# One transfer each way for the diagonal blocks, the decay rows behind them, and a fifth slot for expert weights

## The reference, cut to what matters

```python
# DeltaNet, one chunk: solve with a unit lower triangular matrix, then a recurrence over chunks
A = jnp.where(strict, jnp.einsum('bhnid,bhnjd->bhnij', kb, k) * decay, 0.0)
rhs = jnp.concatenate([v * beta[..., None], kb * jnp.exp(g)[..., None]], -1)
sol = lax.linalg.triangular_solve(eye + A, rhs, left_side=True, lower=True, unit_diagonal=True)
...
def step(S, xs):
    u_n, w_n, qk_n, qd_n, kd_n, gl_n = xs
    v_new = u_n - jnp.einsum('bhcd,bhde->bhce', w_n, S)
    o = jnp.einsum('bhcd,bhde->bhce', qd_n, S) + jnp.einsum('bhij,bhje->bhie', qk_n, v_new)
    S = S * gl_n[..., None, None] + jnp.einsum('bhcd,bhce->bhde', kd_n, v_new)
    return S, o
...
# experts: top two of one group, weighted
hid = jax.nn.silu(jnp.einsum('bld,edf->blef', h, w_gate)) * jnp.einsum('bld,edf->blef', h, w_up)
y = jnp.einsum('blef,efd->bld', hid * combine[..., None].astype(hid.dtype), w_down)
```

## Time and profile before

| | |
|---|---|
| median of three runs | 1129.16 us |
| the profiled execution | 1132.07 us |
| its span, first to last instruction | 1130.3 us |
| TensorE matmuls busy | 814.6 us (72%) |
| TensorE weight loads busy | 486.4 us (43%) |
| VectorE busy | 418.0 us (37%) |
| ScalarE busy | 322.9 us (29%) |
| GpSimd busy | 280.6 us (25%) |
| chain that ended last | PE 34%, DMA 25%, GpSimd 14%, DVE 11% |

### The profile page before, as it was taken

One profiled execution on the slowest core, in us unless ns is written; L12 is line 12 of the kernel. 1 busy time (PEld: TensorE's weight loads), 2 busy tenths in 40 slices (PEclk: granted clock), 3 DMA queues, 4 the chain that ended last, 5 costly groups with the idle time before them and its releaser, 6 DMA issues.

```text
span 1130.3 us, 14986 instructions
## 1 busy us (share of the span) xinstructions
PE 814.6 (72%) x5183; PEld 486.4 (43%) x5183; DVE 418.0 (37%) x1012; ACT 322.9 (29%) x724; POOL 280.6 (25%) x684
## 2 busy tenths in 40 slices
PE   5596658999983439284979689697836944999850
PEld 0253225555541023153656566566635423555430
DVE  0318431111112850252556366464644252111105
ACT  0121313222222222242345254452631021222112
POOL 0000002333321000043626336254360001333220
PEclk8588778999987659588889698888976975999985
DMA  9997299967894982562342513424100085999942
GB/s 345 363 393 298 112 375 358 331 217 282 314 352 146 378 249 75 185 179 37 95 86 53 123 39 94 91 50 122 38 5 6 1 350 207 356 364 350 376 135 111
DMA packets 119779, 227.23 MB, mean 201 GB/s; under 512 B 43421, under 2 KB 85733, under 8 KB 105255
## 3 DMA queue, kind: packets, MB, share of 16 engines
q1 hardware_dynamic: 107232, 198.66, 51.8%
q0 software_dynamic: 8224, 22.56, 6.2%
q10 hardware_dynamic: 4263, 5.21, 1.4%
HBM read 213.25 MB, written 17.33 MB: 204 GB/s over the span
## 4 chain that ended last, share of the span: by engine, by line
PE 34%; DMA 25%; POOL 14%; DVE 11%; issue 5%; SPq 5%; ACT 4%; ACTq 1%; DVEq 0%; POOLq 0%
PE banks L607 10%; DMA h_cols<-in_w_down_dram 7%; POOL arena L982 6%; POOL arena L980 6%; PE banks L619 5%; DMA weight_ring<-in_w_mod_dram 4%; DMA arena<-h_of_tokens,row_now 3%; DMA inverted_blocks<-arena 3%; PE banks L1000 3%; DMA arena<-blocks 3%; PE banks L1714 3%; PE banks L250 2%; SPq L964 2%; PE banks L587 2%; DMA blocks<-arena 2%
## 5 line engine op out<-in xcount | busy, mean ns | idle before, releaser
L1000 PE MATMUL banks<-h_cols,weight_ring 128*128 128x512 f32 (+1 forms) x384 | 166.3, 571 | 0.9 <-ACT modulation L273 0.7
L666 DVE TENSOR_TENSOR arena<-arena,banks 128x128 f32<-128x128 f32 x42 | 12.1, 289 | 235.2 <-ACT arena L635 235.2
L250 PE MATMUL banks<-weight_ring,c_cols 128*32 128x512 f32 x384 | 62.0, 747 | 47.4 <-DMA weight_ring<-in_w_mod_dram 47.1
L1000 PEld LDWEIGHTS banks<-h_cols,weight_ring 128*128 128x128 f32 x384 | 76.0, 215 | 44.0 <-issue 37.5
L702 POOL DMA_INDIRECT y_of_tokens<-arena,place_now x42 | 42.8, 1018 | 195.9 <-ACT arena L642 195.9
L982 POOL TENSOR_TENSOR arena<-arena 128x60 f32<-128x60 f32 (+10 forms) x240 | 78.8, 328 | 18.8
L607 PE MATMUL banks<-weight_ring,arena 128*64 128x256 f32 x640 | 78.8, 403 | 6.4 <-DMA weight_ring<-in_w_down_dram 4.0
L980 POOL TENSOR_TENSOR arena<-arena 128x60 f32<-128x60 f32 (+10 forms) x240 | 78.4, 327 | 18.8
L680 POOL DMA_INDIRECT arena<-h_of_tokens,row_now x50 | 46.3, 925 | 99.4 <-DVE place_of_slot L568 49.0
L630 ACT COPY arena<-arena 64x1024 f32<-64x1024 f32 x46 | 48.1, 1045 | 77.7 <-PE banks L587 57.0
L587 PE MATMUL banks<-const,arena 64*128 64x64 f32 x352 | 57.1, 285 | 12.9 <-ACT arena L630 12.9
(11 more groups left out here) (265 smaller groups left out, 1409.2 us busy)
## 6 DMA issues: line engine op xcount, KB each, us to landing
weight_ring<-in_w_mod_dram SPq DMA_DIRECT2D x48, 1024.0 KB, 12.1
weight_ring<-in_w_gate_dram SPq DMA_DIRECT2D x16, 1024.0 KB, 7.4
weight_ring<-in_w_up_dram SPq DMA_DIRECT2D x16, 1024.0 KB, 10.4
weight_ring<-in_w_down_dram SPq DMA_DIRECT2D x16, 1024.0 KB, 12.7
weight_ring<-in_dn_w_in_dram SPq DMA_DIRECT2D x32, 512.0 KB, 6.6
arena<-in_w_gate_dram SPq DMA_DIRECT2D x8, 1024.0 KB, 12.1
arena<-in_w_up_dram SPq DMA_DIRECT2D x8, 1024.0 KB, 14.4
arena<-in_w_down_dram SPq DMA_DIRECT2D x8, 1024.0 KB, 17.9
```

The source lines that it names most:

```text
L250: mm = pe.matmul(m.ps[j * COL:(j + 1) * COL, 0, :], m.c_cols[:, k, :], w[:, j, :], start=(k == 0), stop=(k == KD - 1))
L1000: mm = pe.matmul(bank(6 + j % 2)[:, 0:CTX + SEQ - n0], head_w[h % 2][:, j, k, :], m.hT[:, k, n0:CTX + SEQ], start=(k == 0), stop=(k == KD ...
```

## The change

- A fifth slot for expert weights, in pieces: two for gate and up (in `modulation` and the second half of `h_cols`), two for down (`modulation`, `mod_sums`). It takes six DMAs instead of three. `expert_loaded` works out the count to wait for; the loop of `sp_moe` is written out for 11 experts.
- The diagonal blocks pass through two compact tiles, `N_diag` and `W_diag`. VectorE and ScalarE copy two quarters each into `N_diag`; one DMA stores it, one DMA loads `W_diag`. ScalarE copies `W_diag` onto the diagonal of `W` (`act_place_blocks`), VectorE transposes straight from `W_diag`. The DRAM layout is now system first, block second.
- `M` is loaded by one DMA whose source is repeated four times.
- SP issues `sp_along` behind `sp_blocks_in`.
- TensorE does five of eight slices of projection 1, then the keys, then the other three. ScalarE takes the squares before the pad of projection 1.
- The arguments of `N` of head x+2 move into recurrence steps 1 and 2, their exponentials to the end of the recurrence, and the third convolution into steps 0 and 1.

```diff
-EXPERT_SLOTS = 4
+EXPERT_SLOTS = 5
...
+        EXPERT_LOADS = [3, 3, 3, 3, 6]
...
+            sp.wait_ge(s("mod_spread"), QUAD * (NQ + 1))
+            sp_expert(sp, L, 4, 4)
             sp.wait_ge(s("router_meta"), L.n + 1)
...
+            for e in range(N_EXPERTS - EXPERT_SLOTS):
+                nt, tb = expert_count(sp, e)
+                sp.wait_ge(s(L.tag + "down"), tb + nt)
+                sp_expert(sp, L, e + EXPERT_SLOTS, e % EXPERT_SLOTS)
...
         def sp_blocks_out(sp, h):
-            sp.wait_ge(s("n_mat"), 2 * (h + 1))
-            for k in range(NB):
-                r = slice(k * BLK, (k + 1) * BLK)
-                sp.dma_start(n_dram[k].rearrange("s r c -> r s c"), N[h % 2][r, :, r]).then_inc(s("n_out"), 16)
+            sp.wait_ge(s("n_mat"), 3 * (h + 1))
+            sp.wait_ge(s("k_length"), 6 * (h + 1))
+            sp.dma_start(n_dram.rearrange("s k r c -> (k r) s c"), N_diag).then_inc(s("n_out"), 16)
 
         def sp_blocks_in(sp, h):
-            sp.wait_ge(s("n_out"), 16 * NB * (h + 1))
-            for g in range(4):
-                sp.dma_start(M[g * BLK:(g + 1) * BLK, :, :], n_dram.rearrange("k s r c -> (k s) r c")).then_inc(s("m_in"), 16)
-            sp.dma_start(U, n_dram.rearrange("k s (q g) c -> g (k s) q c", g=4)).then_inc(s("m_in"), 16)
+            sp.wait_ge(s("n_out"), 16 * (h + 1))
+            sp.dma_start(M, n_dram.rearrange("s k r c -> (s k) (r c)").unsqueeze(0).to_broadcast([4, BLK, BLK * BLK])
+                         ).then_inc(s("m_in"), 16)
+            sp.dma_start(U, n_dram.rearrange("s k (q g) c -> g (s k) q c", g=4)).then_inc(s("m_in"), 16)
...
         def sp_inverse_in(sp, h):
             sp.wait_ge(s("u_out"), 16 * (h + 1))
             if h >= 1:
-                sp.wait_ge(s("o_done"), h)
-            else:
-                sp.wait_ge(s("w_clear"), 2)
-            for k in range(NB):
-                r = slice(k * BLK, (k + 1) * BLK)
-                sp.dma_start(W[r, :, r], w_dram[k].rearrange("s r c -> r s c")).then_inc(s("w_base"), 16)
+                sp.wait_ge(s("v_base"), h)
+                sp.wait_ge(s("joined"), 11 * (h - 1) + 3)
+            sp.dma_start(W_diag, w_dram.rearrange("s k r c -> (k r) s c")).then_inc(s("w_base"), 16)
...
+            if h >= 1:
+                dve.wait_ge(s("n_out"), 16 * h)
+            dve.wait_ge(s("n_mat"), 3 * h + 2)
+            for k in (0, 1):
+                ins = dve.tensor_copy(N_diag[quarter(k), :, :], N[h % 2][quarter(k), :, quarter(k)])
+            ins.then_inc(s("n_mat"), 1)
...
+        def act_place_blocks(act, h):
+            act.wait_ge(s("w_base"), 16 * (h + 1))
...
+            for k in range(NB):
+                ins = act.copy(W[quarter(k), :, quarter(k)], W_diag[quarter(k), :, :])
+            ins.then_inc(s("joined"), 1)
...
         def sp_step(sp, x):
             if closed(x):
                 sp_inverse_out(sp, x)
-            if closed(x) and x + 2 < HEADS:
-                sp_along(sp, x + 2)
-            if closed(x):
                 sp_inverse_in(sp, x)
             if made(x):
                 sp_blocks_out(sp, x + 1)
                 sp_blocks_in(sp, x + 1)
+            if closed(x) and x + 2 < HEADS:
+                sp_along(sp, x + 2)
+            if made(x):
                 sp.wait_ge(s("proj"), proj_made(x + 1, 2))
...
+        V_FIRST = 5
+
         def pe_step(pe, x):
             if made(x):
-                pe_project(pe, x + 1, 1)
+                pe_project(pe, x + 1, 1, 0, V_FIRST)
                 pe_keys(pe, x + 1)
+                pe_project(pe, x + 1, 1, V_FIRST, KD)
...
-            if made(x) and x >= 0:
-                act_exp_n(act, x + 1)
...
             def beside_recur(st):
                 if made(x):
                     act_values(act, x + 1, st)
-                    if st == TT - 1:
+                    if st == TT - 2:
                         act_conv(act, x + 1, 2)
+                if st == TT - 1 and x + 2 < HEADS:
+                    act_exp_n(act, x + 2)
...
             def beside_recur(st):
-                if made(x) and st < 3:
-                    dve_conv(dve, x + 1, 2, 2 * st, min(2 * st + 2, TAPS))
-                if st == 3 and x + 2 < HEADS:
-                    dve_n_args(dve, x + 2)
+                if made(x) and st < 2:
+                    dve_conv(dve, x + 1, 2, 3 * st, min(3 * st + 3, TAPS))
+                if x + 2 < HEADS and st in (1, 2):
+                    dve_n_args(dve, x + 2, *((0, 3), (3, SYS))[st - 1])
```

More of the change, by code:

```diff
@@ new lines, in build, with gate_up, down @@
+        pieces_down = [m.mod[:, 4 * D:5 * D], m.sums.rearrange("p a n -> p (a n)")]
+        EXPERT_LOADS = [3, 3, 3, 3, 6]
+        def gate_up(slot, k):
+            if slot < EXPERT_SLOTS - 1:
+                return whole[slot].rearrange("p a (k f) -> p a k f", k=KD)[:, :, k, :]
+            return pieces[k // (KD // 2)][:, :, k % (KD // 2), :]
+        def down(slot, c):
+            if slot < EXPERT_SLOTS - 1:
+                return whole_down[slot].rearrange("p (c n) -> p c n", c=FC)[:, c, :]
+            return pieces_down[c]
@@ new lines, in sp_expert, with expert_loaded @@
+            w = w_down_flat[n * FE:(n + 1) * FE, :].rearrange("(c p) n -> p c n", p=P)
+            if slot < EXPERT_SLOTS - 1:
+                sp.dma_start(whole_down[slot].rearrange("p (c n) -> p c n", c=FC), w).then_inc(done, 16)
+            else:
+                for c in range(FC):
+                    sp.dma_start(pieces_down[c], w[:, c, :]).then_inc(done, 16)
+        def expert_loaded(L, e):
+            slot = e % EXPERT_SLOTS
+            a_layer = len(range(slot, N_EXPERTS, EXPERT_SLOTS))
+            return s(f"expert_w{slot}"), 16 * EXPERT_LOADS[slot] * (L.n * a_layer + e // EXPERT_SLOTS + 1)
@@ L369, in sp_moe @@
             sp_expert(sp, L, 3, 3)
+            sp.wait_ge(s("mod_spread"), QUAD * (NQ + 1))
+            sp_expert(sp, L, 4, 4)
             sp.wait_ge(s("router_meta"), L.n + 1)
-            with sp.Fori(0, N_EXPERTS // EXPERT_SLOTS - 1) as g:
-                for slot in range(EXPERT_SLOTS):
-                    e = EXPERT_SLOTS * g + slot
-                    nt, tb = expert_count(sp, e)
-                    sp.wait_ge(s(L.tag + "down"), tb + nt)
-                    sp_expert(sp, L, e + EXPERT_SLOTS, slot)
+            for e in range(N_EXPERTS - EXPERT_SLOTS):
+                nt, tb = expert_count(sp, e)
+                sp.wait_ge(s(L.tag + "down"), tb + nt)
+                sp_expert(sp, L, e + EXPERT_SLOTS, e % EXPERT_SLOTS)
         def pe_router(pe, L, beside=lambda: None):
@@ L618, in pe_moe @@
                         for h in range(2):
-                            mm = pe.matmul(column_half(B_DOWN, h), v.hidden[:, f, :], w_d[:, f, h * BANK:(h + 1) * BANK],
+                            mm = pe.matmul(column_half(B_DOWN, h), v.hidden[:, f, :], down(slot, f)[:, h * BANK:(h + 1) * BANK],
                                            start=(f == 0), stop=(f == FC - 1))
@@ L826, in build @@
         QK = [take(256, "p (t n) -> p t n", t=XT) for _ in range(2)]
+        N_diag = take(256, "p (s n) -> p s n", s=SYS)
+        W_diag = take(256, "p (s n) -> p s n", s=SYS)
         P5 = take(256, "p (s n) -> p s n", s=SYS)
@@ L1176, in dve_n, with act_diagonal @@
                 ins.then_inc(s("n_mat"), 1)
+            if h >= 1:
[4 more added lines that the diff above has]
+            ins.then_inc(s("n_mat"), 1)
+        def act_diagonal(act, h):
+            if h >= 1:
+                act.wait_ge(s("n_out"), 16 * h)
+            act.wait_ge(s("n_mat"), 3 * h + 2)
+            for k in (2, 3):
+                ins = act.copy(N_diag[quarter(k), :, :], N[h % 2][quarter(k), :, quarter(k)])
+            ins.then_inc(s("k_length"), 1)
         def dve_q_args(dve, h):
```

91 lines of the change are left out of this document (52 added, 39 removed).

## The result

| | median us | runs | profiled run | its span | granted clock |
|---|---|---|---|---|---|
| before | 1128.92 | 1126.41 to 1130.42, 4 | 1132.07 | 1130.3 | 0.828 |
| after | 1145.08 | 1144.47 to 1148.15, 4 | 1145.27 | 1143.2 | 0.835 |

The ratio is 1.0151, with 95% from 1.0125 to 1.0177: about 16 us slower, where 20 us faster was forecast. The time lies outside the range.

A forecast was written before the change was run, and what follows sets the result against it. A chain of waits through GpSimd, with TensorE close behind, was taken to bound the DeltaNet loop. Experts -17.6 and loop -2.8 gave -20.4 us, a median of 1108.8 us; range 1095.5 to 1120.

The forecast's parts named there:

- The fifth slot: Expert layers: earlier weight loads start the last tile 7.2 us earlier in the first layer, 10.4 in the second; -17.6 together.
- `M` narrows: DeltaNet loop, step (c): the single repeated load takes 6.0 us against 2.25, +3.7 a cycle, bounds -1.2 and +8.2.
- `N_diag` later, TensorE waiting ahead of the keys: DeltaNet loop, engines: TensorE waits 2.6 us before the keys; `N_diag` comes 15.8 us after the recurrence, not 11.4.
- Small transfers (b): GpSimd's chain: one `W_diag` load and one `N_diag` store replace eight transfers, 4.2 us, -5.2; bounds 2.6 and 5.8.
- So there are three rounds: DeltaNet loop: GpSimd's 44.2 us, TensorE's 44.7, a two-head round 45.4 a head; together some 45.8 per interval.
- TensorE's round: DeltaNet loop: TensorE's own cycle per head, 41.3 + 2.9 + 0.5 = 44.7 us.
- second rival: TensorE's new order costs more, as waits lower the clock; a round could hold at 47.5, total 1119 us; chance 0.12.
- The last interval: DeltaNet loop's final GpSimd interval, without decay rows in front: 40.9 becomes 43.0 us, +2.1.
- M stays wide: First rival: `M` loads as wide as before, TensorE's round bounds, total 1094.9 us; chance 0.13.
- The rival on the slower side: Fourth rival: `M` moves at `U`'s 50 GB/s, GpSimd's round is bound alone, total 1135.2 us; chance 0.04.
- a join wait of 1 to 3: Sign in the chain of waits: TensorE's wait before the join is 1 to 3 us instead of 4 to 8.
- the loop's interval: Sign in the DeltaNet loop: the prediction is wrong if the interval between GpSimd's ends stays at 47 us.

The follow-up runs named there:

- mhalves: The changed kernel with `M` in two loads, each with its source repeated twice, instead of one with four repeats: 1187.55 us, ratio 1.0483.
- mwide: The changed kernel with `M` in four separate loads as before, all else as changed: 1101.52 us, ratio 0.9738.
- mwide_order_late: The changed kernel with four `M` loads, the old TensorE and ScalarE order, and the arguments of `N` behind the recurrence: 1083.92 us, ratio 0.9564.
- slots_rowslast: The kernel before with the fifth slot and only the decay rows moved behind `M` and `U`: 1092.05 us, ratio 0.9627.
- mwide_order: The changed kernel with four `M` loads and the old order on TensorE and ScalarE: 1083.33 us, ratio 0.9575.
- mwide_uwide: The changed kernel with `M` in four loads and `U` in four loads and four stores: 1104.14 us, ratio 0.9737.

## Why the prediction was wrong, point by point

**The fifth slot: right in mechanism and near in size.** -17.6 forecast, -15 measured (9 to 21). First layer 6.7 of 7.2. Second layer 7.2 of 10.4, near the lower bound of 7 that was given for gathers on the same engines: each load took 10.8 us and not 10.4, and whether the gathers are why, no run shows. The last two tiles wait 4.56 and 1.35 us for their weights.

**`M` narrows: right in mechanism, too small.** From the store's landing to GpSimd's start I had 10.2 us; it took 11.3 to 12.3. So the term is +5.5 (11.8 and 12.1 against 6.5), not +3.7. I had carried `U`'s share of 0.32, 5.1 engines, over to `M`; the trace of after shows 0.26. The Trainium skill (DMA: Bandwidth & Descriptors, section "Why a DMA increments its semaphore by 16 and not by 1") has the number of engines as the largest up to 16 that divides the slowest dimension of both patterns, by which it is four here and two in mhalves. The traces agree, with DMA shares of 0.26 and 0.13 to 0.19. By that rule the prediction had an estimate of 7.7 us for `M`, and 2.25 + 5.5 = 7.8 was measured.

**`N_diag` later, TensorE waiting ahead of the keys: right.** Forecast 15.8 us after the recurrence and a wait of 2.6; measured 15.9 and 2.65. The 15.8 has a slip in it: `N` moved as the projection did, from 709.3 to 713.4, is ready at 717.7 and not 717.2, which gives 16.3. Undone by itself, with `M` wide, it gives back 2.6 us a round.

**Small transfers (b): the size held, the place didn't.** `W_diag` takes 2.4 us and `N_diag` 2.3. But the two are no longer back to back: the store waits 7.8 us for `N_diag`. The saving of 5.2 us is on a path that has slack.

**The step that failed.** "So there are three rounds" is the sentence. There are four. I wrote that the decay rows "are issued behind `M` and `U`" and took their five microseconds as gone from the queue; I wrote of the arguments in the recurrence only that VectorE has 0.5 us more at step 1. Neither step asked when the rows arrive and when they are wanted. The two edits together close a loop across engines: recurrence, `N_diag`, its store, `M` and `U`, the rows, the arguments in the next recurrence. Behind them stand the terms that I had: 15.9 from the recurrence to `N_diag` and a store of 2.3. The missing ones were 23.6 from the store to the rows and 9.8 from the rows to the end of the recurrence, 2.3 of these the slower clock. Together 51.6 against my 45.8. Easing it at any one of three places takes all or much of the loss of 32 us away: `M` wide (-47 us), arguments behind the recurrence (-31), the old order on TensorE (-18 in the traces). They overlap, since all three shorten or cut the same round; `M` wide brings most, as it shortens GpSimd's too.

Much of this stood in the trace of before. SyncE's and VectorE's timelines there:

```profile
710.31 2.92 SPq L936 DMA_DIRECT2D x_rows<-decay_rows  x2
```
```profile
751.16 1.69 DVE L1131 TENSOR_SCALAR arena<-x_rows,arena 128x128 f32<-128x128 f32 x8
```

The second of the two transfers had landed at 722.4, 12.1 us after the first issue, and was wanted at 751.2: 28.8 us of slack. Counted from GpSimd's end, the change puts the first issue 15.9 us later (16.5 us behind it instead of 0.6) and the use 9.5 us earlier (VectorE is ready for the rows after 31.9 us instead of 41.4). That leaves 3.4 us of slack. What no row of before showed is the rest: the rows land 22.4 us after the first issue instead of 12.1, since SyncE stands 9 us in that issue behind a narrow transfer. 3.4 less 10.3 is -6.9, and VectorE's wait is 6.98. With a wide `M` both issues together take 3.3.

**TensorE's round.** I had 44.7. From the recurrence's end to the join it takes 19.0 us, where I had 17.3: `W_diag` lands at 769.1 but is transposed at 776.08, since the transposes stand on VectorE behind `dve_n` and the copies of `N_diag`. And from the join to the recurrence's end it takes 29.3 to 32.6 us, where I had 27.4; 4.3 to 6.9 of these are TensorE's wait for the rows, and about two the slower clock behind it. The prediction knew that a wait lowers the clock and had it in its second rival, for the waits ahead of the keys and the join; it came in the recurrence, where no wait was forecast.

**The last interval.** I had +2.1, it is +11.7. No rows are loaded in it any more, but its store, at 826.4, still follows the recurrence that had waited for the rows of 800.7; from that store's landing at 829.0 it is 12.3 us to GpSimd's start, and `M` narrow is paid once more.

**The rivals.** "M stays wide" didn't come, but mwide is that case, and its price was good: 1094.9 forecast, 0.9738 x 1128.92 = 1099.3 measured. The rival on the slower side had `M` at `U`'s 50 GB/s and put all of the loss on GpSimd; `M` was not that slow (some 8 us, not 10.5), and GpSimd is not the bound. The time came near its number for another reason. Its chance of 0.04 was that of a mechanism, where it should have been that of "a wait that I haven't seen", which the moves past a queue had earned.

**What the signs said.** I had asked for 10 us from the store to GpSimd and a join wait of 1 to 3; both came (11.8 and 1.39), and both are true of a kernel 36 us slower than forecast. Two signs caught it. From `U`'s landing in DRAM to the store's landing I had asked for 4.2 us, and it was 10.5 in the step shown (766.7 to 777.15), since `N_diag` came so much later than the queue was free. And the loop's interval did not fall below 47: it is 49.0 on average.

**What stays open.** Why SyncE stands in the issue behind a narrow transfer is only argued: its length goes with the pace of the transfer ahead, and no run gave the queue more room. How much of the 8 us between mwide_order_late and slots_rowslast is the compact pieces and how much the earlier third convolution is not settled. Nor is whether decay rows on ScalarE's queue would help at another time.

**The better kernel.** mwide_order keeps the slots, one load and one store for the diagonal pieces, and the rows behind; it takes back the single `M` and the new order. It takes 1083.33 us, 0.9575 of before (0.9517 to 0.9633).

## What to carry to other kernels

When a transfer is moved back in a queue, or its consumer forward, write down the loop that this closes: arrival, consumer, whatever the consumer releases, and so back to the issue. Price that loop like the others, even where the moved transfer looked free. When several transfers are merged into one, look at what the merged pattern has outermost: here one load with four repeats took 5.5 us longer than four loads, and with what was queued behind it that came to 47 us over eight heads. A wait inside a stretch of TensorE's work costs more than its length: behind 6.87 us of waiting came 2.3 us of slower matmuls.

## What the runs showed of the hardware

- The same data on the same target: four loads 6.5 us from the store to GpSimd's start, one load with four repeats outermost 11.8, two loads with two repeats 16.4.
- An issue takes longer behind a narrower transfer: the two issues of the decay rows took 3.3, 10.4 and 13.8 us on SyncE behind these three forms of `M`, and 1.15 us in mwide_uwide, where `U` too was in quarters.
- The decay rows slow small transfers beside them, whichever queue they are on: `W_diag` 8.1 and 10.2 us instead of 2.4, `N_diag`'s store up to 9.3 instead of 2.3. From issue to landing they take 9.9 us in before and 12.9 in after, by the median.
- After 6.87 us of idling in the recurrence TensorE's granted clock was 0.50 for 4.4 us, then 1.00; behind a wait of 1.07 us in mwide it was 1.00 from 763.4 to 769.9.
- Four issues instead of one cost 2.54 us against 0.55 for `U`'s way out; of a landing halved from 4.8 to some 2 us, 0.8 was left.
